# Attention heads: the last elementwise work of GpSimd is given to VectorE

## The chip, the cores and the metric

One core of a Trainium2 chip runs the program. The metric is the device time of one execution in microseconds (us). The kernel before takes 2178.48 us (median of 3 runs, 2176.82 to 2178.69).

## The reference

One encoder layer over 1024 tokens and 16 meta tokens (L = 1040) of width 1024, everything in float32. The part that the change touches is attention over all positions, 8 heads, and the sum of its gated result with that of a recurrent branch:

```
q = (rms_norm(c_q) @ w_uq)   -> q_nope (128), q_rope (64) of each head, rope applied
kv = (rms_norm(c_kv) @ w_ukv) -> k_nope (128), v (128) of each head
s = (q_nope . k_nope + q_rope . k_rope) * scale
a = softmax(s) @ v
mixed = sigmoid(gate_a) * a + sigmoid(gate_h) * r        # r: the recurrent branch
h = h + rms_norm(mixed @ w_o);  h = h + rms_norm(ffn(h))
```

## The kernel before

Every product is made of three matmuls: a float32 operand is split into a rounded high part and a low part (the rest), and `three` (lines 86 to 90) adds high x high, high x low and low x high in one bank. So each operand costs a cast (mostly ScalarE) and a subtraction `x - hi` (VectorE or GpSimd).

Stages follow one another: normalization and the recurrent branch (to about 905 us of the trace), latents and values, the attention heads (about 948 to 1387 us), output product and feed-forward. The change lies in the heads (`attention_heads`, from line 1243).

A head has two halves of 512 queries. Work is in segments. In segment 0 of `both(p, h)` PE projects keys and the first queries of head p (`PIECES` 0 to 4: k, k, k, nope0, rope0), and works on half 0 of head h: transposes of its probabilities (`turn`, k = 0 to 8) and products with the values (`multiply`, k = 0 to 8), with the scores of half 1 of h between them (`score_head` and `score_tail`, j = 0 to 3). In segment 1 PE projects pieces 5 and 6 (nope1, rope1) of head p and works on half 1 of h, with the scores of half 0 of p between. Between the projections and the scores stands `fold` (line 1662), a matmul for the rotary part, which reads `q_turned`.

The engines have one queue each, in program order. On VectorE (line 1509 on) a segment is:

- the pieces' low parts (`piece`, lines 1517 to 1528: `k_nope_lo`, `q_nope_lo`, and `q_turned` = bank x rope table), `low(0)`, `low(1)` (line 1572: the low part of a turned block of probabilities, which `multiply` needs), `fold_low`
- for j = 0 to 3: `find_top(j)` (line 1541, maximum of 784 scores), `low(2j+2)`, `find_shift(j)` (lines 1549 and 1552: maximum of the tail, then the shift of the exponential), `low(2j+3)` up to 7, `normalize(j-1)` (lines 1561 to 1566); at j = 3 also `normalize(3)`
- the gate: line 1612, `mixed = o_bank * gate`

ScalarE computes the exponentials (lines 1442 and 1444) from the shift, casts turned blocks (line 1453), and casts the next head's values (`v_hi`, line 1435, segment 0) and weights (`w_hi`, line 1411, segment 1), both after j = 1. GpSimd follows these two casts with the low parts `v_lo` (line 1387) and `w_lo` (line 1381), and adds the recurrent branch to the gated result (line 1401) after each gate.

PE's waits that matter: `multiply(k)` waits for `low(k)`; `score_head(j)` and `score_tail(j)` wait until ScalarE has read the bank; projection 3 (nope0) waits for the first `k_nope_lo` (it takes the same bank), `fold` for `q_turned`; `turn(0)` waits for all four normalizations.

`begin` (VectorE: line 1617) fills the pipeline for head 0, then come `both(1,0)` to `both(7,6)` (six of them in a loop of two heads a turn) and `both(None, 7)`, in which there is no next head. There the low parts of the first half of `mixed` (line 1578) come in as well.

Of the kernel before, what the change touches and what calls it, by code (L numbers as in the profile page):

```python
# [18 lines left out]
F32 = mybir.dt.float32  # L19
# [3 lines left out]
ALU = mybir.AluOpType  # L23
# [1219 lines left out]
def attention_heads(nc, t, weights, lat, used):  # L1243
# [7 lines left out]
    with ExitStack() as c:  # L1251
# [3 lines left out]
        rec = [sb(f"rec{i}", [P, HALF]) for i in range(2)]  # L1255
# [5 lines left out]
        w_raw, w_hi, w_lo, w_in, w_hi_done, w_lo_done = lat.weights  # L1261
# [9 lines left out]
        v_raw = t.raw[:, QS * L:QS * L + TILES * P].rearrange("p (k m) -> p k m", k=TILES)  # L1271
        v = {(x, i): sb(f"v_{x}{i}", [P, TILES, P], F32R) for x in both_parts for i in range(2)}
# [9 lines left out]
        def mixed(h, i):  # L1282
            return mixed_second[:].unsqueeze(1) if i else lat.mixed_first[:, bass.ds(h.index(), 1), :]
# [19 lines left out]
        v_in, v_hi_done, v_lo_done = signal("av_in", 32), signal("av_hi_done", 1), signal("av_lo_done", 1)  # L1303
# [8 lines left out]
        gated, mix_done = signal("gated", 2), signal("mix_done", 2)  # L1312
# [4 lines left out]
        def iterations(eng, both):  # L1317

            both(At(0), None)
            both(At(1), At(0))  # L1320
            with eng.Fori(0, HEADS // 2 - 1) as j:
                both(At(2, j, 2), At(1, j, 2))
                both(At(3, j, 2), At(2, j, 2))
            both(None, At(HEADS - 1))

        def segments(p, h):

            cur0, cur1 = ((h, 0), (h, 1)) if h is not None else (None, None)
            nxt1 = (p, 0) if p is not None else None
            return (cur0, cur1), (cur1, nxt1)  # L1330

        with nc.Block() as block:
# [36 lines left out]
            @block.gpsimd  # L1369
            def _(pool):  # L1370
                pool.memset(minus_scale[:], -SM_SCALE).then_inc(cleared, 1)
                pool.wait_ge(cleared, 1)
                pool.memset(v_raw[:, TT, :], 0.0).then_inc(cleared, 1)
                pool.wait_ge(cleared, 2)
                for half in range(2):
                    pool.memset(q_rope["lo", half][ROPE:P, :].bitcast(F32), 0.0).then_inc(cleared, 1)
                pool.wait_ge(cleared, 4)

                def weights(at, k):
                    w_hi_done.wait(pool, at, k)  # L1380
                    pool.tensor_tensor(w_lo[:], w_raw[:], w_hi[:].bitcast(F32), ALU.subtract
                                       ).then_inc(w_lo_done.sem, 1)

                def values(p):
                    par = p.base % 2
                    v_hi_done.wait(pool, p, 1)
                    pool.tensor_tensor(v["lo", par][:], v_raw, v["hi", par][:].bitcast(F32), ALU.subtract
                                       ).then_inc(v_lo_done.sem, 1)

                def both(p, h):  # L1390
                    for which, (cur, nxt) in enumerate(segments(p, h)):
                        if p is not None:
                            if which == 0:
                                values(p)
                            else:
                                weights(p, 2)
                        if cur is not None and (p is not None or cur[1] == 0):
                            x, i = cur
                            gated.wait(pool, x, i + 1)
                            gate_in[i].wait(pool, x, 32)  # L1400
                            pool.tensor_tensor(mixed(x, i), mixed(x, i), rec[i][:].unsqueeze(1), ALU.add
                                               ).then_inc(mix_done.sem, 1)

                iterations(pool, both)

            @block.scalar
            def _(act):
                def weights(at, k):
# [98 lines left out]

            @block.vector
            def _(dve):
                def piece(p, i):  # L1510

                    name, _, _, _, a, w, src = PIECES[i]
                    if i in BY_ACT:
                        piece_hi.wait(dve, p, BY_ACT.index(i) + 1)
                    if name == "k":
                        par = p.base % 2
                        dve.tensor_tensor(k_nope["lo", par][:, key_at(a, w)], src[:, 0:w],
                                          k_nope["hi", par][:, key_at(a, w)].bitcast(F32),
                                          ALU.subtract).then_inc(piece_read.sem, 1)
                        return  # L1520
                    half = int(name[-1])
                    if name.startswith("nope"):
                        dve.tensor_tensor(q_nope["lo", half][:], src, q_nope["hi", half][:].bitcast(F32),
                                          ALU.subtract).then_inc(piece_read.sem, 1)
                    else:
                        piece_done.wait(dve, p, i + 1)
                        fold_done.wait(dve, p, half)
                        dve.tensor_tensor(q_turned[:], src, table[:, a:a + w],
                                          ALU.mult).then_inc(piece_read.sem, 1)
# [26 lines left out]
                def normalize(nxt, j):  # L1556
                    x, i = nxt
                    e = i * QS + j
                    col = slice(j, j + 1)
                    exp_done.wait(dve, x, e + 1)  # L1560
                    dve.tensor_tensor(inv[i][:, col], sums[i][:, col], sums_tail[i][:, col], ALU.add
                                      ).then_inc(sum_done.sem, 1)
                    sum_done.wait(dve, x, e + 1)
                    dve.reciprocal(inv[i][:, col], inv[i][:, col]).then_inc(inv_done.sem, 1)
                    inv_done.wait(dve, x, e + 1)
                    dve.tensor_scalar(prob[i][:, j, :], prob[i][:, j, :], inv[i][:, col], None, ALU.mult
                                      ).then_inc(p_done.sem, 1)
# [13 lines left out]
                def segment(cur, nxt, p, which):  # L1581
                    last = p is None
                    if p is not None:
                        for i in OF_SEGMENT[which]:
                            piece(p, i)
                    if cur is not None:
                        low(cur, 0)
                        low(cur, 1)
                    if p is not None:
                        fold_low(p, which)  # L1590
                    for j in range(QS):
                        if nxt is not None:
                            find_top(nxt, j)
                        if cur is not None:
                            low(cur, 2 * j + 2)
                        if nxt is not None:
                            find_shift(nxt, j)
                        if cur is not None and 2 * j + 3 < TILES:
                            low(cur, 2 * j + 3)
                        if nxt is not None and j:  # L1600
                            normalize(nxt, j - 1)
                        if nxt is not None and j == QS - 1:
                            normalize(nxt, j)
                        if last:
                            split_low(which * QS + j)
                    if cur is not None:
                        h, i = cur
                        pv_done.wait(dve, h, (i + 1) * TILES)
                        gate_in[i].wait(dve, h, 32)
                        if i:  # L1610
                            mixed_out.wait(dve, h, 16, lag=1)
                        dve.tensor_tensor(mixed(h, i), o_bank[:].unsqueeze(1), gate[i][:].unsqueeze(1), ALU.mult
                                          ).then_inc(gated.sem, 1)

                dve.wait_ge(cleared, 4)

                def begin(p):
                    for i in range(NP_ - 1):
                        piece(p, i)
                    fold_low(p, 0)  # L1620
                    piece(p, NP_ - 1)
                    fold_low(p, 1)
                    for j in range(QS):
                        find_top((p, 0), j)
                        find_shift((p, 0), j)
                        if j:
                            normalize((p, 0), j - 1)
                    normalize((p, 0), QS - 1)

                def both(p, h):  # L1630
# [1354 lines left out]
```

## Time and profile before

| | |
|---|---|
| median of the runs | 2178.48 us |
| profiled execution | 2178.05 us, its span 2176.3 us |
| PE busy (matmul) | 2125.7 us, 98%, 11536 instructions |
| VectorE busy | 1283.7 us, 59%, 1966 instructions |
| ScalarE busy | 948.1 us, 44% |
| GpSimd busy | 398.4 us, 18%, 242 instructions |
| granted TensorE clock | 0.997 of full |

Busy PE is a modelled figure, since matmuls overlap: each of 512 columns is shown as 0.39 us long, but the next one starts 0.23 us later. Times of a row are its start and its length; where a bracket stands behind, the engine was idle that long before it, and the instruction named released it. The profiled execution lies 1.75 us above its span.

### The profile page before, as it was taken

The page shows a single profiled execution, that of the slowest core. Times are in us where ns is not written, and L with a number is a line of the kernel's source. Part 1 is how long each engine was busy: PE and PEld are TensorE (multiplying, and loading weights), DVE is VectorE, ACT ScalarE, POOL GpSimd, SP SyncE. Part 2 cuts the span into 40 slices and gives each one's busy share as a digit, 9 for nine tenths or more (in the row PEclk, how much of TensorE's full clock was granted, in tenths as well). Part 3 has the DMA queues.
Part 4 walks back from the last instruction along what each step waited for, and adds up shares of the span by engine and source line. Part 5 has one row for each costly group of instructions (what it writes and reads, how often), then busy time and mean ns, then how long its engine had stood idle before and what let it go on. Part 6 is the DMA issues. An engine that isn't in the chain of part 4 may idle for free. (4 is left out here: it accounts for less than half of the span.)

```text
span 2176.3 us, 30857 instructions
## 1 busy us (share of the span) xinstructions
PE 2125.7 (98%) x11536; PEld 1796.0 (83%) x11536; DVE 1283.7 (59%) x1966; ACT 948.1 (44%) x1550; POOL 398.4 (18%) x242
## 2 busy tenths in 40 slices
PE   8999999999999999989999999999999999999999
PEld 8988888888888888778888888777788888888886
DVE  3403664756647557447777777568866766651431
ACT  6324354443554525455555555545432323243422
POOL 1110000000000000021111111020055454524443
PEclk9999999999999999999999999999999999999999
DMA  5112111120120111130111111254322222354452
GB/s 187 60 54 68 35 64 51 47 68 34 63 68 34 63 56 41 49 137 1 49 48 51 47 50 42 102 192 148 129 83 78 97 79 73 122 183 164 148 184 96
DMA packets 79101, 181.82 MB, mean 84 GB/s; under 512 B 6976, under 2 KB 27776, under 8 KB 77344
## 3 DMA queue, kind: packets, MB, share of 16 engines
q1 hardware_dynamic: 79008, 180.56, 23.8%
q8 instruction: 61, 1.00, 0.2%
q14 instruction: 32, 0.26, 0.0%
HBM read 142.13 MB, written 38.40 MB: 83 GB/s over the span
## 5 line engine op out<-in xcount | busy, mean ns | idle before, releaser
L88 PE MATMUL h_bank<-hn_hi,w_hi 128*128 128x512 f32 (+2 forms) x952 | 371.0, 390 | 2.8 <-ACT raw L716 1.6
L90 PE MATMUL h_bank<-hn_hi,w_lo 128*128 128x512 f32 (+2 forms) x952 | 353.4, 371 | 0.0
L89 PE MATMUL h_bank<-hn_lo,w_hi 128*128 128x512 f32 (+2 forms) x952 | 353.0, 371 | 0.0
L88 PEld LDWEIGHTS h_bank<-hn_hi,w_hi 128*128 128x128 f32 x952 | 179.0, 188 | 33.2 <-issue 8.7
L90 PEld LDWEIGHTS h_bank<-hn_hi,w_lo 128*128 128x128 f32 x952 | 178.7, 188 | 27.7
L89 PEld LDWEIGHTS h_bank<-hn_lo,w_hi 128*128 128x128 f32 x952 | 179.2, 188 | 26.5 <-issue 3.8
L716 ACT COPY raw<-h_bank 128x512 f32<-128x512 f32 (+2 forms) x119 | 63.8, 543 | 279.8 <-PE h_bank L90 249.4
L2148 ACT CAST w_hi<-w_raw 128x1024 fp32r<-128x1024 f32 x79 | 82.7, 1049 | 203.7 <-PE f_bank L90 192.9
L895 DVE TENSOR_TENSOR w_lo<-w_raw,w_hi 128x1024 fp32r<-128x1024 f32 x52 | 63.5, 1221 | 138.2 <-ACT w_hi L696 138.2
L1132 POOL MEMSET ckv_hi<- 128x224 f32 x1 | 0.3, 284 | 778.8 <-POOLq L585 778.8
L1453 ACT CAST prob_hi<-a_bank 128x512 fp32r<-128x512 f32 x144 | 83.1, 588 | 131.5 <-PE a_bank L1721 131.1
L2118 POOL TENSOR_TENSOR w_lo<-w_raw,w_hi 128x1024 fp32r<-128x1024 f32 x45 | 108.4, 2409 | 144.2 <-ACT w_hi L2148 144.2
L88 PE MATMUL f_bank<-ffn_in_hi,w_hi 128*128 128x512 f32 x320 | 127.0, 397 | 6.3 <-DVE w_lo L2437 5.4
L89 PE MATMUL f_bank<-ffn_in_lo,w_hi 128*128 128x512 f32 x320 | 124.6, 389 | 0.0
L90 PE MATMUL f_bank<-ffn_in_hi,w_lo 128*128 128x512 f32 x320 | 124.6, 389 | 0.0
L2123 POOL TENSOR_TENSOR set_lo<-combos,set_hi 128x512 fp32r<-128x512 f32 x72 | 98.7, 1372 | 88.8 <-ACT set_hi L2211 88.8
L1572 DVE TENSOR_TENSOR prob_lo<-a_bank,prob_hi 128x512 fp32r<-128x512 f32 x144 | 97.9, 689 | 24.6 <-ACT prob_hi L1453 20.8
L88 PE MATMUL f_bank<-t_hi,set_hi 128*128 128x512 f32 x288 | 112.0, 389 | 0.0
L89 PE MATMUL f_bank<-t_lo,set_hi 128*128 128x512 f32 x288 | 112.0, 389 | 0.0
L90 PE MATMUL f_bank<-t_hi,set_lo 128*128 128x512 f32 x288 | 112.0, 389 | 0.0
L2211 ACT CAST set_hi<-combos 128x512 fp32r<-128x512 f32 x72 | 44.5, 618 | 100.0 <-PE f_bank L90 66.5
L88 PE MATMUL f_bank<-t_hi,w_hi 128*128 128x512 f32 x224 | 87.7, 391 | 0.0
(411 smaller groups left out, 5374.1 us busy)
## 6 DMA issues: line engine op xcount, KB each, us to landing
w_raw<-in_w_ffn SPq DMA_DIRECT2D x82, 512.0 KB, 3.5
w_raw<-in_w_hgrn SPq DMA_DIRECT2D x54, 512.0 KB, 3.2
raw_up<-in_w_ffn SPq DMA_DIRECT2D x18, 512.0 KB, 4.6
hidden<-gate_blocks SPq DMA_DIRECT2D x34, 256.0 KB, 2.0
w_raw<-in_w_out SPq DMA_DIRECT2D x15, 512.0 KB, 3.3
w_raw<-in_w_head SPq DMA_DIRECT2D x9, 512.0 KB, 5.7
X<-in_x SPq DMA_DIRECT2D x8, 520.0 KB, 9.0
values<-values_h SPq DMA_DIRECT2D x32, 128.0 KB, 1.7
```

The lines of the kernel that those rows point to most:

```text
L88: pe.matmul(out, wh, xh, start=start, stop=False)
L89: pe.matmul(out, wh, xl, start=False, stop=False)
L90: return pe.matmul(out, wl, xh, start=False, stop=stop)
L716: act.copy(t.raw[:, s * L + a:s * L + a + w], bank[made.banks[e]][:, 0:w]).then_inc(proj_copied.sem, 1)
L895: dve.tensor_tensor(w_lo[s % 2][:], w_raw[s % 2][:], w_hi[s % 2][:].bitcast(F32), ALU.subtract).then_inc(w_lo_done.sem, 1)
L1132: pool.memset(part[:, :, L:].bitcast(F32), 0.0).then_inc(padded, 1)
L1453: act.copy(turned_hi[k % RING][:], turn_bank[k % 2][:]).then_inc(p_hi.sem, 1)
L1572: dve.tensor_tensor(turned_lo[k % RING][:], turn_bank[k % 2][:], turned_hi[k % RING][:].bitcast(F32), ALU.subtract).then_inc(p_lo.sem, 1)
L2118: pool.tensor_tensor(w_lo[b % 2][:], w_raw[b % 2][:], w_hi[b % 2][:].bitcast(F32), ALU.subtract).then_inc(w_lo_done, 1)
L2123: pool.tensor_tensor(set_lo[:, i], product_source(mat, i), set_hi[:, i].bitcast(F32), ALU.subtract).then_inc(set_lo_done, 1)
L2148: act.copy(w_hi[b % 2][:], w_raw[b % 2][:]).then_inc(w_hi_done, 1)
L2211: act.copy(set_hi[:, i], product_source(mat, i)).then_inc(set_hi_done, 1)
```

## The change

GpSimd's three operations of the heads go to VectorE. The low part of the values is placed in segment 0 after `normalize(1)` (j = 2), before `find_top(3)`; that of the weights at the same place of segment 1; in `begin` they stand after j = 1 and after j = 2. The addition of the recurrent branch stands behind the gate, with a wait for the gate's own completion in front. As before, the last half of the last head is not added here (line 2517 does it). GpSimd keeps only the memsets ahead of the heads. The waits of the other engines stay as they are, on the same semaphores. The new code in `weights` also waits for VectorE's own earlier `w_lo`.

```diff
@@ gpsimd
-                def weights(at, k):
-                    w_hi_done.wait(pool, at, k)
-                    pool.tensor_tensor(w_lo[:], w_raw[:], w_hi[:].bitcast(F32), ALU.subtract
-                                       ).then_inc(w_lo_done.sem, 1)
-
-                def values(p):
-                    par = p.base % 2
-                    v_hi_done.wait(pool, p, 1)
-                    pool.tensor_tensor(v["lo", par][:], v_raw, v["hi", par][:].bitcast(F32), ALU.subtract
-                                       ).then_inc(v_lo_done.sem, 1)
...
-                            gated.wait(pool, x, i + 1)
-                            gate_in[i].wait(pool, x, 32)
-                            pool.tensor_tensor(mixed(x, i), mixed(x, i), rec[i][:].unsqueeze(1), ALU.add
-                                               ).then_inc(mix_done.sem, 1)
...
@@ vector
+                def weights(p):
+                    w_hi_done.wait(dve, p, 2)
+                    w_lo_done.wait(dve, p, 1)
+                    dve.tensor_tensor(w_lo[:], w_raw[:], w_hi[:].bitcast(F32), ALU.subtract
+                                      ).then_inc(w_lo_done.sem, 1)
+
+                def values(p):
+                    par = p.base % 2
+                    v_hi_done.wait(dve, p, 1)
+                    dve.tensor_tensor(v["lo", par][:], v_raw, v["hi", par][:].bitcast(F32), ALU.subtract
+                                      ).then_inc(v_lo_done.sem, 1)
...
                         if nxt is not None and j:
                             normalize(nxt, j - 1)
+                        if j == 2 and p is not None:
+                            if which == 0:
+                                values(p)
+                            else:
+                                weights(p)
                         if nxt is not None and j == QS - 1:
                             normalize(nxt, j)
...
                         dve.tensor_tensor(mixed(h, i), o_bank[:].unsqueeze(1), gate[i][:].unsqueeze(1), ALU.mult
                                           ).then_inc(gated.sem, 1)
+                        if p is not None or i == 0:
+                            gated.wait(dve, h, i + 1)
+                            dve.tensor_tensor(mixed(h, i), mixed(h, i), rec[i][:].unsqueeze(1), ALU.add
+                                              ).then_inc(mix_done.sem, 1)
...
                         if j:
                             normalize((p, 0), j - 1)
+                        if j == 1:
+                            values(p)
+                        elif j == 2:
+                            weights(p)
```

## Rows read from the trace of the kernel before

**Rows 1.** Windows, heads: us, busy (count) per engine, PEclk, DMA, GB/s.
```profile
943.00:1390.00 447.00, 433.56 (x2457) 371.42 (x2456) 330.96 (x625) 226.92 (x486) 61.07 (x35) 0.99 0.14 45
```

**Rows 2.** Timeline of PE, segment 1 to segment 0: start, length, instruction, idle before.
```profile
1085.52 0.50 PE L88 MATMUL a_scores<-cq_hi,w_hi 128*128 128x512 f32 x1 [0.30 <-DVE k_nope_lo L1517]
```

**Rows 3.** Timeline of PE, segment 0 to segment 1.
```profile
1109.79 0.39 PE L88 MATMUL a_bank<-prob_hi,v_hi 128*128 128x512 f32 x1
...
1115.50 1.12 PE L1669 MATMUL a_bank<-q_turned,consts 128*128 128x512 f32 x2
```

**Rows 4.** Timeline of VectorE, end of segment 0, start of segment 1.
```profile
1105.10 1.10 DVE L1552 SCALAR_TENSOR_TENSOR shift<-top,top_tail,minus_scale 128x1 f32<-128x1 f32 x1
1106.12 0.68 DVE L1572 TENSOR_TENSOR prob_lo<-a_bank,prob_hi 128x512 fp32r<-128x512 f32 x1
...
1107.10 0.76 DVE L1566 TENSOR_SCALAR prob<-prob,inv 128x1040 f32<-128x1040 f32 x1
1107.78 0.97 DVE L1541 TENSOR_REDUCE top<-a_scores 128x1 f32<-128x784 f32 x1
1108.66 0.68 DVE L1572 TENSOR_TENSOR prob_lo<-a_bank,prob_hi 128x512 fp32r<-128x512 f32 x1
...
1114.75 0.69 DVE L1528 TENSOR_TENSOR q_turned<-a_scores,rope_table 128x512 f32<-128x512 f32 x1 [0.73 <-PE a_scores L90]
```

**Rows 5.** Timeline of VectorE in the recurrent branch: the same subtraction there.
```profile
332.19 1.22 DVE L895 TENSOR_TENSOR w_lo<-w_raw,w_hi 128x1024 fp32r<-128x1024 f32 x1
333.32 0.42 DVE L797 TENSOR_TENSOR factor_b<-cum_b 128x256 f32<-128x256 f32 x1
```

**Rows 6.** Timeline of VectorE, end of segment 1, start of segment 0.
```profile
1076.85 0.71 DVE L1552 SCALAR_TENSOR_TENSOR shift<-top,top_tail,minus_scale 128x1 f32<-128x1 f32 x1
1077.48 0.68 DVE L1572 TENSOR_TENSOR prob_lo<-a_bank,prob_hi 128x512 fp32r<-128x512 f32 x1
...
1078.46 0.76 DVE L1566 TENSOR_SCALAR raw<-raw,inv 128x1040 f32<-128x1040 f32 x1
1079.30 0.97 DVE L1541 TENSOR_REDUCE top<-a_scores 128x1 f32<-128x784 f32 x1
1080.36 0.69 DVE L1572 TENSOR_TENSOR prob_lo<-a_bank,prob_hi 128x512 fp32r<-128x512 f32 x1
...
1083.25 0.16 DVE L1561 TENSOR_TENSOR inv<-sums,sums_tail 128x1 f32<-128x1 f32 x1 [0.46 <-ACT raw L1444]
...
1084.32 0.69 DVE L1612 TENSOR_TENSOR mixed_second<-a_bank,w_raw 128x512 f32<-128x512 f32 x1
1084.92 1.03 DVE L1517 TENSOR_TENSOR k_nope_lo<-a_scores,k_nope_hi 128x384 fp32r<-128x384 f32 x2
```

**Rows 7.** Timeline of GpSimd: two operations of a head.
```profile
1075.15 2.40 POOL L1381 TENSOR_TENSOR w_lo<-w_raw,w_hi 128x1024 fp32r<-128x1024 f32 x1 [13.46 <-ACT w_hi L1411]
...
1103.51 2.67 POOL L1387 TENSOR_TENSOR v_lo<-raw,v_hi 128x1152 fp32r<-128x1152 f32 x1 [17.15 <-ACT v_hi L1435]
```

**Rows 8.** Timelines of VectorE and PE in begin.
```profile
965.02 1.46 DVE L1552 SCALAR_TENSOR_TENSOR shift<-top,top_tail,minus_scale 128x1 f32<-128x1 f32 x1
...
968.02 0.39 PE L1678 MATMUL a_bank<-k_nope_hi,q_nope_hi 128*128 128x256 f32 x1 [2.14 <-ACT raw L1444]
```

**Rows 9.** View of line 1552, the shift: length in ns, shortest, median, longest.
```profile
L1552 DVE SCALAR_TENSOR_TENSOR shift<-top,top_tail,minus_scale x64: 219/221/1456, 965.0 to 1369.8; 128x1 f32<-128x1 f32 x64
```

**Rows 10.** Timelines of VectorE and PE between the last head's two segments.
```profile
1372.76 1.33 PE L1721 MATMUL a_bank<-consts,prob 128*128 128x128 f32 x5 [1.30 <-DVE prob L1566]
...
1373.22 0.69 DVE L1612 TENSOR_TENSOR mixed_first<-a_bank,w_raw 128x512 f32<-128x512 f32 x1
1373.89 0.69 DVE L1572 TENSOR_TENSOR prob_lo<-a_bank,prob_hi 128x512 fp32r<-128x512 f32 x1
```

**Rows 11.** Windows, columns as in rows 1: in begin, and around the last segment's start.
```profile
966.00:967.00 1.00, 0.00 (x0) 0.00 (x0) 1.00 (x2) 0.49 (x1) 0.46 (x1) 1.00 1.17 277
1372.00:1380.00 8.00, 6.69 (x25) 5.46 (x26) 5.26 (x8) 2.97 (x7) 1.27 (x1) 0.57 0.01 2
```

More of the change, by code:

```diff
@@ L1377, in _ @@
                 pool.wait_ge(cleared, 4)
-                def weights(at, k):
-                    w_hi_done.wait(pool, at, k)
-                    pool.tensor_tensor(w_lo[:], w_raw[:], w_hi[:].bitcast(F32), ALU.subtract
-                                       ).then_inc(w_lo_done.sem, 1)
-                def values(p):
-                    par = p.base % 2
-                    v_hi_done.wait(pool, p, 1)
-                    pool.tensor_tensor(v["lo", par][:], v_raw, v["hi", par][:].bitcast(F32), ALU.subtract
-                                       ).then_inc(v_lo_done.sem, 1)
[L1390 to L1398, printed above, removed]
-                            gated.wait(pool, x, i + 1)
-                            gate_in[i].wait(pool, x, 32)
-                            pool.tensor_tensor(mixed(x, i), mixed(x, i), rec[i][:].unsqueeze(1), ALU.add
-                                               ).then_inc(mix_done.sem, 1)
-                iterations(pool, both)
             @block.scalar
```

## The prediction, made before the result

> **What bounds the kernel now.** I read the page's busy shares first, then the windows of the stage that the change touches, then the waits by engine, and last the timelines of all engines over one head. The windows view of the heads says that PE is busy 433.56 of 447 us there, VectorE 330.96 and GpSimd 61.07 [rows 1]. PE bounds the stage; VectorE has 116 us to spare in it, and an account by busy time alone would say that the 31 us or so of new work fit in. What decides is where VectorE's spare time lies, so the reader should look in the timeline for what each instruction waited for. Early in a segment VectorE waits for PE; at its end it is PE that is only just served. Two places show this. Projection 3 of segment 0 already waits for `k_nope_lo` (0.30 us, at 1085.52) [rows 2]. The `fold` of segment 1 starts at 1115.50 [rows 3], and `q_turned`, which it reads, ended at 1114.75 + 0.69 = 1115.44 [rows 4]: served with 0.06 us to spare. And from j = 2 on VectorE runs without idle time: `find_top(3)` starts at 1107.78, right when the normalization ahead of it (1107.10) lets it [rows 4]. So the new work is put at the point where VectorE has just lost its slack, and behind it stand the shift of the last exponential, the last normalization, the gate, and only then the operations that PE waits for.
>
> **The change part by part.**
>
> *Prices.* The same subtraction of 1024 elements, both inputs in SBUF, takes VectorE 1.22 us, and the next instruction starts 1.13 us after it (332.19 to 333.32) [rows 5]. A 512-element one is 0.69 long with the next after 0.60 (1084.32 to 1084.92) [rows 6]. That is 1.04 ns an element, so the 1152 elements of `v_lo` hold the queue for 1.13 + 0.13 = 1.26 us. The addition has to wait for the gate's end, 0.69 us after its start, and for the signal, for which I take 0.05 us from the 0.06 between `q_turned`'s end and PE's `fold` [rows 3, 4]; then it holds the queue for another 0.60. In place of 0.60 from the gate to the next instruction there are 1.34: it costs 0.74 us. Bounds: 0.60 if the wait costs nothing, 0.9 if address arithmetic for the indexed `mixed_first` comes on top.
>
> *What GpSimd gives back.* GpSimd's `v_lo` runs from 1103.51 to 1106.18 [rows 7]. The tiny shift of VectorE (one element a partition) starts at 1105.10 in this time and lasts 1.10 us, to 1106.20 [rows 4]. `w_lo` ends at 1075.15 + 2.40 = 1077.55 [rows 7], the shift at 1076.85 + 0.71 = 1077.56 [rows 6]. Both times the shift ends with GpSimd's operation, so it was held by it; in begin, where GpSimd makes `w_lo` too, one lasts 1.46 us [rows 8]. Without it I expect 0.22 us, the median of all 64 shifts [rows 9]. What is released is not all of that, for `low(7)`, next in the queue, waits for a cast of ScalarE too. In segment 1 it started 0.63 us after the shift did (1077.48), and in segment 0 it took 1.02 us (1106.12) [rows 4, 6]. With the cast alone to wait for it should take about 0.61, so VectorE gains 0.02 us in segment 1 and 0.41 in segment 0.
>
> The Trainium skill, page "SBUF — State Buffer", section "Who interferes with whom", says the same of the mechanism: a VectorE instruction with two SBUF inputs and a GpSimd instruction that reads SBUF exclude each other for their whole length. By that rule the hold goes in all places, which is the sum below; if the page and these rows were wrong about the cause, the sum would be that of the rival "nothing is given back".
>
> *Segment 1 to segment 0 (the weights, then the addition, then `k_nope_lo`), 6 times.* The normalization at 1078.46 lets the next instruction start 0.68 later (as 1107.10 to 1107.78) [rows 4, 6], at 1079.14, less the 0.02; `find_top(3)` now starts at 1079.12 + 1.13 = 1080.25 in place of 1079.30, 0.95 later. `low(8)` may follow 0.88 after it (1107.78 to 1108.66) [rows 4]; before it came 1.06 after it (1080.36), held by its cast [rows 6], so it swallows 0.18: it is 0.77 late. The shift of j = 3 and the last exponential are late by the full 0.77, and the last normalization waits for that exponential already (0.46 us idle at 1083.25) [rows 6], so it passes the 0.77 on; what PE loses before that, waiting for `low(8)`, is inside it. Then the addition: 0.77 + 0.74 = 1.51 us late for `k_nope_lo`, and PE's projection 3, which waits for it today, is as late. **1.5 us each, 9.0 in all.** Bounds 1.2 to 1.8 (addition 0.6 to 0.9, and 0.2 either way for the cast in front of `low(8)`).
>
> *Segment 0 to segment 1 (the values, then the addition, then `q_nope_lo` and `q_turned`), 7 times.* `find_top(3)` is late by 1.26 - 0.41 = 0.85. No idle time lies between it and the gate that would not move with it, so the gate is 0.85 late and `q_nope_lo` 1.59. In front of `q_turned` are 0.73 us of idle time, and 0.08 more by which instructions overlap [rows 4]. So `q_turned` is late by 0.78, and `fold` with it. `multiply(8)` at 1109.79 stood 0.45 behind `low(8)` (1108.66 + 0.68) [rows 3, 4], so PE is 0.4 to 0.5 late from there, inside the 0.78. **0.8 us each, 5.6 in all.** Bounds 0.5 (PE's own lateness only) to 1.0.
>
> *The last head, once each.* After the last `both` with a next head come no projections; `turn(0)` waits for the last normalization, 0.77 late. The addition there lies beside the transposes and scores, in which PE has 2 us of other work. Between the last two segments the gate starts at 1373.22 and `low(0)` follows at 1373.89 without idle time [rows 10]; the addition moves it by 0.67, and nothing but this chain is left for PE. **1.4 us**, bounds 0.7 to 2.5, since this stretch runs partly at the lower clock already, a mean of 0.57 over 8 us [rows 11].
>
> *Begin.* The first shift ends at 965.24 in place of 966.48 [rows 8, 9], so the first exponential and PE's tail scores (968.02, after 2.14 us of waiting [rows 8]) come 1.24 earlier. Values and weights then put 1.26 and 1.13 in the way of `find_top(2)` and `find_top(3)`. I followed them in the timeline: the 1.24, and some 0.4 of idle time in front of each tail maximum, pay for both, and the last shift stays where it was. **0**, bounds -1.2 (the gain reaches PE) to 1.0 (the idle time doesn't help).
>
> *At nothing.* `v_lo` and `w_lo` are ready some 2.5 us later in their segment than by GpSimd, but PE needs `w_lo` first at the next segment's projections (about 2 us behind its new end) and `v_lo` a whole head later. Uncovered, `w_lo` would cost what it is late. SP's loads of values, weights and gates wait for these semaphores, and each is issued more than 10 us ahead of its reader. GpSimd's additions took 1.29 us and let no one wait. The wait of VectorE for its own `w_lo` is met a head earlier. The new wait with a queue behind it is that for the gate, and it is in the price of the addition.
>
> *Sum.* 9.0 + 5.6 + 1.4 + 0 = 16.0 us on the profiled execution's own 2178.05 (span 2176.3 and 1.75 around it): **2194.0 us**, 0.7% slower. The profiled execution lies 0.4 us under the median of the runs, which is inside their spread. By the bounds: 7.2 + 3.5 + 0.7 - 1.2 = 10.2 to 10.8 + 7.0 + 2.5 + 1.0 = 21.3, that is 2188.3 to 2199.4.
>
> **The rivals.**
>
> *The spare time swallows it (not slower).* One mechanism: VectorE's 116 us of idle time in the heads [rows 1] take up the 31 us, and the lifted hold in begin shortens PE's wait by 1.24 us [rows 8]: 2176.8 us. It decides if `find_top(3)` has 1.26 us of slack in front of it. The rows say 0.1 at most [rows 4, 6]. 3%, and 2% more that half of it is swallowed on a path that I read as taut (2184 to 2188).
>
> *Nothing is given back.* If the shift is slow for another reason than GpSimd's operation, segment 0 is 0.41 later (7 x 0.41 = 2.9) and begin about 0.9 later: 2194.0 + 3.8 = 2197.8 us. Against it: two pairs of ends that agree to 0.02 us [rows 4, 6, 7]. 5%.
>
> *The clock falls.* Between the last head's segments PE pauses for 1.30 us (and for less before and behind) [rows 10], and the granted clock over the 8 us from 1372 shows 0.57: most of them were spent at 1.2 GHz in place of 2.4, which costs PE 8 x 0.43 = 3.4 us [rows 11]. The change makes a pause of about 1.5 us, shortly after one of 0.35, at six places. If each lets the clock fall: 6 x 3.4 = 20.4 more, 2214 us; if one does, 2197. Against it: in begin PE stands still for 2.14 us [rows 8] and the window in its midst still shows 1.00 [rows 11]. 7% for one that passes the range. The Trainium skill ("TensorE: Matmul & The Clock Gate", Part 1) has idleness as the ground on which the clock is gated to 1.2 GHz; by it both outcomes are open here, since the pauses are short.
>
> **How the numbers follow.** Forecast 83%, nothing given back 5%, clock 7%, swallowed wholly or half 5%. The range, 2188 to 2200.5, is the sum's bounds and reaches over the second rival; it leaves out the clock rival and the swallowed one, and some of the forecast's own error. A measurement can tell about 0.2% (4.4 us) from no change, so slower means above 2182.8: 0.96; the same 0.03; faster 0.01, for it would need 4.4 us of gain where PE has 13 us of idle time in the whole stage [rows 1].
>
> **What would show it.** Step by step: `v_lo` on VectorE of 1.35 us and `w_lo` of 1.22; all shifts near 0.22 us; PE waits for `k_nope_lo` of some 1.5 us six times, for `q_turned` or `prob_lo` of 0.3 to 0.5 us seven times each; a head lasting 2.3 us longer; everything outside the heads as before. Wrong if a head's length grows by less than 1.5 us or more than 3, if the shift stays long, or if the clock shows 0.5 in a segment boundary.

## The result, and the profile after

The changed kernel takes 2191.66 us (median of 4 runs, 2189.95 to 2192.01), the kernel before 2178.40 beside it: a ratio of 1.0064, with a 95% interval of 1.0052 to 1.0076. It is 13.3 us slower, where 16.0 were forecast; 2191.7 lies in the range. The profiled execution took 2191.93 us, its span is 2190.1.

The page's first lines (span; busy time of each engine, its share, its instructions), then the windows view of the heads, which answers [rows 1], and the view of the shift, which answers [rows 9]:

```profile
span 2190.1 us, 30828 instructions
PE 2130.1 (97%) x11536; PEld 1794.5 (82%) x11536; DVE 1300.1 (59%) x1997; ACT 946.7 (43%) x1550; POOL 338.6 (15%) x211
```
```profile
943.00:1401.00 458.00, 435.37 (x2448) 368.11 (x2446) 346.45 (x655) 224.19 (x484) 1.29 (x4) 0.99 0.14 43
```
```profile
L1537 DVE SCALAR_TENSOR_TENSOR shift<-top,top_tail,minus_scale x64: 219/220/223, 964.8 to 1383.2; 128x1 f32<-128x1 f32 x64
```

GpSimd has only its memsets left in the heads. VectorE is busy 15.5 us longer there, not 31. The 64 shifts are all at 0.22 us now, which gives 10.8 us of busy time back (389 to 220 ns in the mean). Most of the rest is overlap: instructions that follow one another directly overlap by some 0.08 us in the records, and the view counts that time once. VectorE still idles for 112 of 458 us, and the stage is longer all the same.

VectorE's timeline at the end of segment 0 and the start of segment 1 (start, length, instruction, idle before), to be read beside [rows 4]:

```profile
1109.01 0.22 DVE L1537 SCALAR_TENSOR_TENSOR shift<-top,top_tail,minus_scale 128x1 f32<-128x1 f32 x1
1109.60 0.69 DVE L1557 TENSOR_TENSOR prob_lo<-a_bank,prob_hi 128x512 fp32r<-128x512 f32 x1 [0.37 <-ACT prob_hi L1426]
...
1110.59 0.76 DVE L1551 TENSOR_SCALAR prob<-prob,inv 128x1040 f32<-128x1040 f32 x1
1111.27 1.35 DVE L1492 TENSOR_TENSOR v_lo<-raw,v_hi 128x1152 fp32r<-128x1152 f32 x1
1112.54 0.97 DVE L1526 TENSOR_REDUCE top<-a_scores 128x1 f32<-128x784 f32 x1
1113.42 0.68 DVE L1557 TENSOR_TENSOR prob_lo<-a_bank,prob_hi 128x512 fp32r<-128x512 f32 x1
...
1117.29 0.68 DVE L1602 TENSOR_TENSOR mixed_first<-a_bank,w_raw 128x512 f32 x1
1118.01 0.69 DVE L1606 TENSOR_TENSOR mixed_first<-mixed_first,rec 128x512 f32 x1
1118.62 0.68 DVE L1508 TENSOR_TENSOR q_nope_lo<-a_scores,q_nope_hi 128x512 fp32r<-128x512 f32 x1
1119.27 0.69 DVE L1513 TENSOR_TENSOR q_turned<-a_scores,rope_table 128x512 f32<-128x512 f32 x1
```

The reader should see three things. `low(7)` starts 0.59 after the shift (before: 1.02). `v_lo` holds the queue for 1.27 us and `find_top(3)` follows it without idle time. And the 0.73 us of idle time that stood in front of `q_turned` are used up.

The end of segment 1, beside [rows 6], and what PE makes of both ends, beside [rows 2, 3]:

```profile
1136.70 1.22 DVE L1486 TENSOR_TENSOR w_lo<-w_raw,w_hi 128x1024 fp32r<-128x1024 f32 x1
1137.83 0.97 DVE L1526 TENSOR_REDUCE top<-a_scores 128x1 f32<-128x784 f32 x1
...
1142.58 0.68 DVE L1602 TENSOR_TENSOR mixed_second<-a_bank,w_raw 128x512 f32<-128x512 f32 x1
1143.30 0.69 DVE L1606 TENSOR_TENSOR mixed_second<-mixed_second,rec 128x512 f32<-128x512 f32 x1
1143.91 1.03 DVE L1502 TENSOR_TENSOR k_nope_lo<-a_scores,k_nope_hi 128x384 fp32r<-128x384 f32 x2
```
```profile
1113.46 0.39 PE L90 MATMUL a_bank<-prob_hi,v_lo 128*128 128x512 f32 x1
1114.16 0.50 PE L88 MATMUL a_bank<-prob_hi,v_hi 128*128 128x512 f32 x1 [0.31 <-DVE prob_lo L1557]
1114.49 0.39 PE L89 MATMUL a_bank<-prob_lo,v_hi 128*128 128x512 f32 x1
...
1120.02 1.12 PE L1667 MATMUL a_bank<-q_turned,consts 128*128 128x512 f32 x2
...
1144.51 0.50 PE L88 MATMUL a_scores<-cq_hi,w_hi 128*128 128x512 f32 x1 [1.28 <-DVE k_nope_lo L1502]
```

PE's two longest waits in the heads (waiting line, whom for: us in total, times, longest):

```profile
PE a_scores L88 <- DVE k_nope_lo L1502: 8.3, 7, 1.3
PE a_bank L88 <- DVE prob_lo L1557: 3.5, 15, 0.3
```

The first was 2.5 us before, the second 0.2.

### The profile page after: what moved, and what is told of

It reads as the page before. It is cut to its first block and busy times, and to the rows that moved or that the text cites. A ratio compares the mean times of both kernels' runs of the same rounds, so it can differ in the third digit from the quotient of the medians.

```text
span 2190.1 us, 30828 instructions
## 1 busy us (share of the span) xinstructions
PE 2130.1 (97%) x11536; PEld 1794.5 (82%) x11536; DVE 1300.1 (59%) x1997; ACT 946.7 (43%) x1550; POOL 338.6 (15%) x211
```

## The experiments

Two theories went in. *Place*: a new instruction costs what is left of it after the slack between it and the next instruction that PE waits for. *Load*: VectorE's added work costs in proportion, 13.3 us for 31 us of instructions, wherever it stands (0.43 us for each us). Each kernel is set against runs of the kernel before beside it (2177.7 to 2178.4 us). To see the two ends of a head apart, the table gives, for the third head of each profiled execution, the time from the start of `k_nope_lo` to that of `q_turned` of segment 1 (first end) and from there to the next head's `k_nope_lo` (second end), each as the difference from the kernel before, where they are 1114.75 - 1084.92 = 29.83 [rows 4, 6] and 23.22 us.

| kernel | first end | second end | time, us | ratio to before, 95% interval |
|---|---|---|---|---|
| changed kernel | +0.60 | +1.42 | 2191.66 | 1.0064 (1.0052 to 1.0076) |
| additions only | +0.01 | +0.74 | 2182.81 | 1.0024 (1.0015 to 1.0033) |
| low parts only | +0.65 | +0.69 | 2187.32 | 1.0041 (1.0027 to 1.0054) |
| low parts at j = 2, additions late | +0.59 | +0.69 | 2186.49 | 1.0039 (1.0026 to 1.0053) |
| all at covered places | -0.02 | 0.00 | 2177.64 | 1.0002 (0.9993 to 1.0011) |
| the same, low parts' work doubled | 0.00 | +0.01 | 2177.97 | 0.9998 (0.9989 to 1.0007) |
| changed kernel, doubled at j = 2 | +1.88 | +2.56 | 2210.19 | 1.0146 (1.0129 to 1.0163) |
| changed kernel, GpSimd reads | +1.09 | +1.54 | 2197.37 | 1.0089 (1.0075 to 1.0103) |
| kernel before, gate late | +0.04 | -0.61 | 2174.35 | 0.9984 (0.9975 to 0.9994) |
| all covered, gate late | +0.03 | -0.59 | 2174.51 | 0.9982 (0.9973 to 0.9991) |

### The two parts alone

Additions only (the kernel before, with GpSimd's `tensor_tensor(..., ALU.add)` and its waits taken out):

```diff
                         dve.tensor_tensor(mixed(h, i), o_bank[:].unsqueeze(1), gate[i][:].unsqueeze(1), ALU.mult
                                           ).then_inc(gated.sem, 1)
+                        if p is not None or i == 0:
+                            gated.wait(dve, h, i + 1)
+                            dve.tensor_tensor(mixed(h, i), mixed(h, i), rec[i][:].unsqueeze(1), ALU.add
+                                              ).then_inc(mix_done.sem, 1)
```

> The kernel before, with only the 15 additions of the recurrent branch moved to VectorE, right behind the gate; GpSimd keeps the low parts. Theory of place (what counts is how much slack lies between the new instruction and the next one that PE waits for): ahead of k_nope_lo there is none, 6 x 0.73 us; ahead of q_turned there is 0.81 us of slack and the addition takes 0.57, so nothing is lost there; the last head loses 0.4. Together 4.8 us: 2183.2 us. Theory of load (VectorE's added busy time costs in proportion, 13.3 us for 31 us): 10.4 us added cost 4.5 us: 2182.9 us. The total can't tell them apart, the timeline can: by place the fold of segment 1 does not move relative to the preceding k_nope_lo, and k_nope_lo of the next head does, by 0.73 us.

Measured: 2182.81 us, and the timeline is that of place: nothing at the first end, 0.74 at the second. One and the same instruction is free at one end of the segment and costs its whole price at the other.

Low parts only (the changed kernel; its additions are taken out of VectorE's queue and GpSimd's block for them is put back as it was):

> The changed kernel with the additions given back to GpSimd: only the low parts of values and weights are on VectorE. Theory of place: in front of segment 1 the slack before q_turned takes up the 0.85 us of lateness but PE itself loses about 0.4 us waiting for the low part of block 8 (7 x 0.4 = 2.8 to 3.1); in front of segment 0 the 0.69 us go through in full (6 x 0.69 = 4.1), the last head 0.7, begin -0.2: 7.7 us, 2186.1 us. Theory of load: 20.6 us added cost 8.8 us: 2187.2 us.

Measured: 2187.32 us, 1.2 more than place gave and at load's figure. The second end is +0.69 as expected. The first is +0.65, where 0.4 stood. In this kernel VectorE waits for PE again in front of `q_turned`:

```profile
1115.91 0.68 DVE L1519 TENSOR_TENSOR q_nope_lo<-a_scores,q_nope_hi 128x512 fp32r<-128x512 f32 x1
1117.32 0.69 DVE L1524 TENSOR_TENSOR q_turned<-a_scores,rope_table 128x512 f32<-128x512 f32 x1 [0.73 <-PE a_scores L90]
```

So the 0.65 is PE's own lateness, which begins at `multiply(8)`. The rows of the changed kernel above show its parts. Without a wait `multiply(8)` would start 0.23 after 1113.46, at 1113.69; it starts at 1114.16, 0.47 late, though the bracket says 0.31. Its next matmul comes 0.33 after it in place of 0.23, which is 0.1 more. A bracket of 0.31 stands for a loss of 0.57. That is most of the 0.65; the other 0.08 is not traced.

Low parts at j = 2 with the additions on VectorE, but behind the three `k_nope_lo` of the next segment 0 and behind `q_nope_lo` in segment 1:

> The changed kernel (low parts at j = 2), with the additions on VectorE but at covered places: behind the three k_nope_lo of the next segment 0 and behind q_nope_lo in segment 1. Theory of place: the additions then cost nothing, so it runs as the kernel in which GpSimd keeps them: 2187.3 us, a head 1.32 us longer than before. Theory of load: VectorE has the full 31 us more, 2191.7 us.

Measured: 2186.49 us, both ends as where GpSimd makes the additions. Load is 5 us off here. An addition in VectorE's queue is free if it stands a few instructions later.

### The same work where VectorE waits

```diff
@@ scalar: segment
                     if p is not None:
                         fold_high(p, which)
+                        if which == 0:
+                            values(p)
+                        else:
+                            weights(p, 2)
...
-                        if j == 1 and p is not None:
-                            if which == 0:
-                                values(p)
-                            else:
-                                weights(p, 2)
@@ vector: segment
+                    if which == 0:
+                        if p is not None:
+                            for i in range(3):
+                                piece(p, i)
...
+                            add_it(h, 1, 1)
+                        if p is not None:
+                            for i in range(3, 5):
+                                piece(p, i)
+                    else:
+                        if p is not None:
+                            piece(p, 5)
+                        add_it(h, 0, 0)
+                        if p is not None:
+                            piece(p, 6)
...
                             low(cur, 2 * j + 3)
+                        if j == 0 and p is not None:
+                            if which == 0:
+                                values(p)
+                            else:
+                                weights(p)
...
-                        if j == 2 and p is not None:
...
```

Here `add_it` is the addition with its wait, taken from behind the gate.

> All of the work stays on VectorE, but each piece stands where VectorE waits for PE in the trace: the low part of values or weights at the end of j = 0, ahead of find_top(1) (1.17 us idle there, plus 0.37 in front of low(5)), with ScalarE's cast of them moved from after j = 1 to before the j loop; the addition behind the three k_nope_lo of the next segment 0 (2.2 us idle follow) and behind q_nope_lo in segment 1 (0.7 us idle follow). Theory of place: all is covered, and the time is that of the kernel before, 2178 us, within 1.5. Theory of load: the same 31 us are added, so it stays where the changed kernel is, 2191.7 us.

Measured: 2177.64 us, no difference from the kernel before, with the same instructions on VectorE as in the changed kernel. Its timeline in segment 0:

```profile
1094.77 0.69 DVE L1556 TENSOR_TENSOR prob_lo<-a_bank,prob_hi 128x512 fp32r<-128x512 f32 x1 [0.37 <-ACT prob_hi L1426]
1095.38 1.35 DVE L1491 TENSOR_TENSOR v_lo<-raw,v_hi 128x1152 fp32r<-128x1152 f32 x1
1096.65 0.97 DVE L1525 TENSOR_REDUCE top<-a_scores 128x1 f32<-128x784 f32 x1
```

`v_lo` lies exactly in the 1.17 us in which VectorE waited for the scores. This decides against load: 31 us at nothing. ScalarE's casts of values and weights had to move as well, ahead of the j loop; that move was not run by itself, but the two doublings below differ in the place alone from the kernels that they are set against.

How much such a place holds, and how little the other one does, was asked by doubling. Ahead of each low part a useless subtraction of the same size goes in (of two constant tiles, into a tile of its own), once at the covered place and once at j = 2 of the changed kernel:

```diff
                             if which == 0:
+                                again(p, 0, LK)
                                 values(p)
                             else:
+                                again(p, 1, KT * P)
                                 weights(p)
```

> The kernel with all of VectorE's new work at covered places, and at the end of j = 0 of each segment a second, useless subtraction of the same size (1152 or 1024 elements of two constant tiles): 17 us more VectorE work. Theory of place: 1.26 us come on top of a gap of 1.17 that the first one fills, but waits of 0.37 in front of low(5) and low(7), and 0.18 in front of low(6), take most of it up before find_top(3): at most 0.2 us a segment are left, 2178 to 2180 us. Theory of load: 17 x 0.43 = 7 us more, 2185 us.

> The changed kernel with a second, useless subtraction of the same size ahead of each low part at j = 2. Theory of place: there is no slack behind that point, so each passes in full: 7 x 1.26 + 6 x 1.13 + 1.13 = 16.7 us more, 2208.4 us. Theory of load: 17 x 0.43 = 7 us more, 2199 us. It also makes PE's stops longer, to 1.9 and 2.6 us with the refill: if pauses of this length let the clock fall, the granted clock shows 0.5 in the boundaries and the time goes beyond 2212 us.

Measured: 2177.97 us at the covered place, nothing, and 2210.19 us at j = 2, 18.5 us above the changed kernel, where 16.7 were expected. The first end grew by 1.28 and the second by 1.14, the two holding times being 1.26 and 1.13, so the queue gives the 16.7; the rest is the clock, shown below. The timeline of the covered kernel shows where the second copy goes:

```profile
1095.44 1.35 DVE L1486 TENSOR_TENSOR spare<-ckv_lo 128x1152 f32<-128x1152 f32 x1
1096.71 1.35 DVE L1498 TENSOR_TENSOR v_lo<-raw,v_hi 128x1152 fp32r<-128x1152 f32 x1
1097.98 0.97 DVE L1532 TENSOR_REDUCE top<-a_scores 128x1 f32<-128x784 f32 x1
...
1104.12 0.69 DVE L1563 TENSOR_TENSOR prob_lo<-a_bank,prob_hi 128x512 fp32r<-128x512 f32 x1 [0.26 <-ACT prob_hi L1428]
```

`find_top(1)` is 1.3 us late, and at the `low(7)` of 1104.12 VectorE waits for its cast again: the lateness has run out before `find_top(3)`. Of the kernel doubled at j = 2, PE's wait at the first end and the windows view of the heads:

```profile
1119.29 0.50 PE L88 MATMUL a_bank<-prob_hi,v_hi 128*128 128x512 f32 x1 [1.58 <-DVE prob_lo L1564]
```
```profile
943.00:1420.00 477.00, 436.84 (x2443) 369.62 (x2442) 363.65 (x669) 223.78 (x484) 1.29 (x4) 0.99 0.13 41
```

PE stands still for 1.58 us at one place and 1.25 to 1.3 at the others, over and over, and the granted clock is 0.99 of full in the mean over the stage, as before and in the changed kernel. The mean hides one difference. Where the last head begins there are no projections between PE's waits, and there the clock fell. PE's waits at this place, and windows of the kernel doubled at j = 2:

```profile
1376.33 0.50 PE L88 MATMUL a_bank<-prob_hi,v_hi 128*128 128x512 f32 x1 [1.31 <-DVE prob_lo L1564]
1377.99 0.45 PE L1728 MATMUL a_bank<-consts,raw 128*128 128x128 f32 x1 [0.47 <-DVE raw L1558]
1379.61 0.69 PE L1728 MATMUL a_bank<-consts,raw 128*128 128x128 f32 x2 [1.17 <-DVE raw L1558]
```
```profile
1374.00:1378.00 4.00, 2.22 (x12) 1.33 (x11) 3.83 (x8) 1.10 (x3) 0.00 (x0) 1.00 0.00 0
1380.00:1382.00 2.00, 2.00 (x8) 1.73 (x7) 1.85 (x4) 1.17 (x2) 0.00 (x0) 0.50 0.05 20
```

The changed kernel has waits of 0.17, 0.47 and 1.29 us at the same place, and its clock stays at 1.00 there. From the turn at 1379.61 (1363.82 in the changed kernel) to the scores at 1387.29 (1369.06) the doubled kernel takes 7.68 in place of 5.24 us, so this one fall cost 2.4 us. The profiled execution, 2211.02 us, is the changed kernel's 2191.93 plus 16.7 plus 2.4. The 19 pauses of 1.25 to 1.58 us ahead of this place did not bring the clock down.

### GpSimd's hold on the shift

```diff
@@ gpsimd, in the changed kernel
+                def idle_work(p, k, n):
+                    spared.wait(pool, p, k)
+                    pool.tensor_tensor(spare[:, 0:n], ckv["lo"][:, 1, 0:n].bitcast(F32),
+                                       ckv["lo"][:, 0, 0:n].bitcast(F32), ALU.subtract).then_inc(spared.sem, 1)
...
+                                v_hi_done.wait(pool, p, 1)
+                                idle_work(p, 0, LK)
...
+                                w_hi_done.wait(pool, p, 2)
+                                idle_work(p, 1, KT * P)
```

> The changed kernel, with GpSimd doing a useless subtraction of two constant SBUF tiles of the same size at the moments when it made v_lo and w_lo before; nobody waits for it. If GpSimd's reading is what held VectorE's one-element shift: the shift of j = 2 lasts until GpSimd ends (1.1 us in segment 0, 0.7 in segment 1, 1.4 in begin), segment 0 loses 0.41 us seven times and begin 1.2: 4.1 us more than the changed kernel, 2195.8 us. If the shift was long for another reason (who reads v_lo and w_lo, the semaphores, the order of the queue): all shifts stay at 0.22 us and the time at 2191.7 us.

Measured: 2197.37 us, 5.7 above the changed kernel. GpSimd's row, and the shift of the same moment:

```profile
1108.55 2.68 POOL L1383 TENSOR_TENSOR spare<-ckv_lo 128x1152 f32<-128x1152 f32 x1 [27.46 <-ACT v_hi L1427]
```
```profile
1109.60 0.42 DVE L1553 TENSOR_REDUCE top_tail<-a_bank 128x1 f32<-128x256 f32 x1
1110.06 1.19 DVE L1556 SCALAR_TENSOR_TENSOR shift<-top,top_tail,minus_scale 128x1 f32<-128x1 f32 x1
```

GpSimd ends at 1111.23, the shift at 1111.25, and nobody waits for the work that GpSimd did. It is GpSimd's operation, not the data, that holds it. The maximum in front, whose input is a bank, ran in the same time at its usual 0.42 us. The cost is 0.49 us at the first end and 0.12 at the second, 3.4 + 0.7 us, and in begin the shift of 1.45 us is back, and the first `k_nope_lo` behind it is 1.6 us later (19.49 in place of 17.85 us after the last `q_turned` of begin). That would add up to the 5.7, but not all of the 1.6 is the hold's. In this profile the granted clock fell to the lower level in begin, behind PE's pause of 2.14 us. It did so in the kernel with the additions only as well, whose begin is that of the kernel before, after the same pause (2.13 us, ended at 966.96), where the kernel before itself shows 1.00:

```profile
968.00:970.00 2.00, 2.00 (x8) 1.71 (x7) 1.49 (x5) 1.44 (x4) 0.00 (x0) 0.50 0.97 355
```

There the same stretch was 0.92 us longer than in the kernel before, and 1.01 longer in the kernel before with the gate late, where the clock fell too. So 0.6 to 0.7 us of the 1.6 are left for the hold, an estimate from these differences, and 3.4 + 0.7 + 0.7 = 4.8 us for all of it. Whether the other executions, whose median gives the 5.7, had this fall is not known. The Trainium skill ("SBUF — State Buffer", "Who interferes with whom") has the exclusion for VectorE's two SBUF inputs against a GpSimd instruction that reads SBUF; this run agrees. Its other half, that a GpSimd operation which only writes does not hold VectorE, no run here shows.

### The gate behind `k_nope_lo`

In the heads of the kernel before, PE waited for `k_nope_lo` 7 times, 2.5 us in all: 0.30 us at each of six starts of a segment 0 [rows 2], and 0.68 once, behind begin. The one thing in front of it that PE does not need yet is the gate of the second half.

```diff
@@ vector: segment, in the kernel before
+                    if which == 0 and p is not None:
+                        for i in range(3):
+                            piece(p, i)
+                    if which == 0 and not (cur[0].j is None and cur[0].base == 0):
+                        gate_it(cur[0], 1, 1)
...
-                        pv_done.wait(dve, h, (i + 1) * TILES)
-                        ...
+                        if i == 0 or last:
+                            gate_it(h, i, 0)
```

> The kernel before (GpSimd keeps all three kinds of work), with one thing changed: the gate of a head's second half stands behind the three k_nope_lo of the next segment 0 in place of ahead of them. Theory of place: k_nope_lo is 0.60 us earlier, PE's stop in front of projection 3 (0.30 idle in the row, some 0.5 with what the overlapping records hide) goes: 6 x 0.5 = 3 us faster than the kernel before, ratio 0.9986. Theory of load: VectorE's work is the same, no change.

> All of the work on VectorE at covered places, and the gate of the second half behind k_nope_lo as well. Theory of place: the same 3 us below the kernel before, ratio 0.9986, with GpSimd free. Theory of load: 2191.7 us.

Measured: 2174.35 us with GpSimd's work left where it was (10 runs), 2174.51 with all of it on VectorE at covered places (11 runs); before 2177.92 in the same runs. Both intervals end below 1. In the first of the two, VectorE and then PE at the boundary:

```profile
1083.66 0.55 DVE L1517 TENSOR_TENSOR k_nope_lo<-a_scores,k_nope_hi 128x384 fp32r<-128x384 f32 x1
...
1085.35 0.68 DVE L1584 TENSOR_TENSOR mixed_second<-a_bank,w_raw 128x512 f32<-128x512 f32 x1
```
```profile
1084.41 0.39 PE L88 MATMUL a_scores<-cq_hi,w_hi 128*128 128x512 f32 x1
```

The matmul is 0.39 long and has no bracket: the stop is gone. A head is 0.57 us shorter (52.69 against 53.26 us over the last five), 3.4 us in six. These are the two fastest kernels of the study; whether GpSimd helps in them makes no difference that can be measured.

## Why the prediction was right

The sign, the mechanism (a queue place behind VectorE's slack) and the places of the losses came out as the prediction put them; at one of the two ends of a head, what carried the loss was another of the two paths that it named. The sum was 2.2 us too high on the spans (16.0 against 2190.1 - 2176.3 = 13.8). No term was too low, so the closeness is not owed to errors that cancel. By its terms:

- *Begin*, 0 forecast: the first `k_nope_lo` of the next head came 0.20 us earlier (978.45 to 978.25), of which 0.06 lie ahead of the heads. The lifted hold and the idle time paid for both low parts.
- *Segment 0 to segment 1*, 7 x 0.8 = 5.6 forecast: the seven ends grew by 0.60 to 0.67, 4.5 in all. Here a step was mis-sized. I took 0.60 us from the gate to the next instruction and 1.34 with the addition, from the gate of segment 1. At the gate of segment 0 the follower came 0.76 us behind it already before the change, because it waited for ScalarE's cast, which ended at 1112.71 + 0.59 = 1113.30:

```profile
1112.57 0.68 DVE L1612 TENSOR_TENSOR mixed_first<-a_bank,w_raw 128x512 f32 x1
1113.33 0.69 DVE L1523 TENSOR_TENSOR q_nope_lo<-a_scores,q_nope_hi 128x512 fp32r<-128x512 f32 x1
```
```profile
1112.71 0.59 ACT L1425 CAST q_nope_hi<-a_scores 128x512 fp32r<-128x512 f32 x1 [1.24 <-PE a_scores L90]
```

  With the addition it is 1118.62 - 1117.29 = 1.33. So from the gate on 0.57 us were added, not 0.74: 0.16 us of slack in front of `q_nope_lo` were overlooked. Address arithmetic for the indexed `mixed_first`, which the prediction had as something that might come on top, shows nowhere: with the low parts only, where the gate is later and the cast is done by its end, the follower of the same indexed gate comes after 0.60 us (1115.31 to 1115.91).
- In the same term, PE's own lateness from `low(8)` was put at 0.4 to 0.5, "inside the 0.78". It is 0.6, and the experiments show that it alone is the loss: with the additions on GpSimd or placed late the first end is the same. In the changed kernel the two paths arrive together, so my reason for this term, the addition in front of `q_turned`, was the wrong one of two that I named; by itself the addition there costs nothing (+0.01). Its lower bound, 0.5, had been given to PE's lateness.
- *Segment 1 to segment 0*, 6 x 1.5 = 9.0 forecast: 1.39 to 1.42 each, 8.4 in all. The addition's share of 0.74 was measured as 0.74; the low part's was forecast as 0.77 and is 0.69. `top_tail` followed `low(8)` by 0.59 us (1138.72 to 1139.31), by 0.68 before (1080.36 to 1081.04), where VectorE had waited ahead of it.
- *The last head*, 1.4 forecast: 1.0. The last normalization passed on its 0.67 us, and the addition 0.64 of its 0.67: PE's next group starts at 1388.68 in place of 1374.64, 14.04 later, where the turn ahead of it was 13.40 later (1386.16, 1372.76). But 0.29 us of this come back where the clock rises again. PE before, then after:

```profile
1374.64 1.12 PE L1721 MATMUL a_bank<-consts,prob 128*128 128x128 f32 x4 [0.55 <-DVE prob_lo L1572]
...
1378.97 0.91 PE L1721 MATMUL a_bank<-consts,prob 128*128 128x128 f32 x4
1379.63 0.47 PE L88 MATMUL a_bank<-prob_hi,v_hi 128*128 128x512 f32 x1
```
```profile
1386.16 1.31 PE L1719 MATMUL a_bank<-consts,prob 128*128 128x128 f32 x5 [1.29 <-DVE prob L1551]
1388.68 1.11 PE L1719 MATMUL a_bank<-consts,prob 128*128 128x128 f32 x4 [1.22 <-DVE prob_lo L1557]
...
1393.01 0.62 PE L1719 MATMUL a_bank<-consts,prob 128*128 128x128 f32 x4
1393.38 0.47 PE L88 MATMUL a_bank<-prob_hi,v_hi 128*128 128x512 f32 x1
```
```profile
1386.00:1394.00 8.00, 6.63 (x26) 5.35 (x27) 5.17 (x9) 3.21 (x6) 0.00 (x0) 0.57 0.01 2
```

The stretch at the lower clock is as long as before (0.57 over 8 us, as in [rows 11]) and begins at the same turn. PE waits through more of it, so less of its work falls into it: the last of these turns takes 0.37 us to its follower in place of 0.66. A wait inside a stretch at the lower clock is partly paid back.

A head lasted 2.04 us longer in the mean of the last five (55.30 against 53.26), 2.3 forecast.

Of the rivals, the spare time did not swallow the work (though it does elsewhere in the segment: the covered kernels). "Nothing is given back" is out, since all shifts are short after the change and become long when GpSimd reads. The clock did not fall in the changed kernel at any place where it had not fallen before. But pauses of about this length can bring it down: with the work at j = 2 doubled it fell at one place more. And the argument against it, that the window in the midst of begin's pause of 2.14 us shows 1.00, held for one execution; behind the same pause the clock fell in the profiles of the additions-only and the gate-late kernel. For the operations at nothing no wait has appeared for `v_lo` or `w_lo` on PE, ScalarE or VectorE. SP's queue waits once for `v_lo`, 14.8 us where it was 6.5, and once 0.7 us for `w_lo`, and no engine waits longer for a load through it (ScalarE for the values: 0.5 us in all, 0.6 before).

## What to carry to other kernels

On an engine that is not the bound, a new instruction costs its queue time minus the slack behind it, not a share of the load: 31 us of work cost 13.3 us at one place and nothing at another, with the low parts some 10 us earlier in the same segment and the additions a few instructions later, and another 17 us at the low parts' new place were free as well. Look in the timeline for the last idle time ahead of the place and for the next instruction that the bounding engine waits for; what stands in front of that instruction without being needed yet (here the gate) is worth moving by itself. When PE's wait is costed from its bracket, add what the overlapping records hide and the slow restart. And read the granted clock in narrow windows behind each pause, since the mean over a stage (0.99 with one stretch at the lower clock, and 0.99 with two) doesn't show a fall.

## What the runs showed of the hardware

- A VectorE instruction of one element a partition with its inputs in SBUF lasts as long as a GpSimd subtraction beside it goes on: 1.10, 0.71 and 1.46 us in place of 0.22. GpSimd's share of the busy time hides this, since the lost time is booked to VectorE: 10.8 us in the heads.
- PE's idle time in a bracket is too short by what successive matmuls overlap: 0.31 us in the bracket were 0.47 of delay, and 0.57 with the restart (the matmul after the stop came 0.33 us behind it, not 0.23).
- A wait of VectorE for its own last instruction cost 0.04 us beyond its end (gate 1142.58 + 0.68, addition 1143.30).
- TensorE kept its 2.4 GHz in the kernel doubled at j = 2 through 19 pauses of 1.25 to 1.58 us, 5 to 26 us apart (granted clock 1.00 up to 1378). It fell to 1.2 GHz there behind pauses of 1.31, 0.47 and 1.17 us within 5 us (0.50 from 1380 to 1384), which cost 2.4 us.
- The same code and the same pause do not always meet the same clock: behind a pause of 2.13 to 2.14 us in begin it stayed at 1.00 in the profile of the kernel before and fell to 0.50 in those of the additions-only and the gate-late kernel, which cost 0.9 to 1.0 us.
